# Repacking the latent-attention q, the rotary key and the delta-rule q/k norms of one long fp32 kernel

## What is computed

```python
q = q * rsqrt(sum(q*q) + eps) * 128**-0.5      # per token and head, 128 features
k = k * rsqrt(sum(k*k) + eps)
```

```python
q = (_rms_norm(c_q, q_norm) @ w_uq).reshape(B, S, 8, 96)     # c_q has 384 features
q = concatenate([q[..., :64], _rope(q[..., 64:], positions)])
k_pe = broadcast(_rope(k_rope, positions), 8 heads)          # k_rope = h @ w_kr, 32 features
_rope(t): t1, t2 = halves of 16; concat([t1*cos - t2*sin, t2*cos + t1*sin])
```

## Time and profile before

| | us |
|---|---|
| median of 3 runs (lowest, highest) | 2778.39 (2776.52, 2786.57) |
| the profiled execution, its own time | 2773.64 |
| its span in the trace | 2771.8 |
| PE, DVE, ACT, POOL busy in it | 2631.3, 1504.0, 935.1, 368.4 |

### The profile page before, as it was taken

The page is one execution under the profiler, slowest core; times in us unless marked ns, Lnnn a source line. Parts: engine busy times, 40 slices in busy tenths (PEclk is TensorE's granted clock), DMA queues, the critical chain, the costliest instruction groups (busy, mean ns, idle before and its releaser), DMA issues.

```text
span 2771.8 us, 36466 instructions
## 1 busy us (share of the span) xinstructions
PE 2631.3 (95%) x14714; PEld 1817.7 (66%) x14714; DVE 1504.0 (54%) x2935; ACT 935.1 (34%) x2234; POOL 368.4 (13%) x277
## 2 busy tenths in 40 slices
PE   6899999999999899999999899999999999999997
PEld 3567767667676576646544346677767663888886
DVE  2487786887877636534342445433475222677722
ACT  2436456465473531032342233222233212222100
POOL 0221121220221000000000121222032210000031
PEclk8999999999999999999999999999999999999999
DMA  5221321312213425121001031111322121122220
GB/s 234 76 43 45 91 60 45 81 29 83 60 44 92 134 90 218 56 99 46 15 31 38 26 100 61 61 61 61 137 76 85 52 91 61 61 91 92 84 84 31
DMA packets 108649, 209.78 MB, mean 76 GB/s; under 512 B 82433, under 2 KB 88385, under 8 KB 96961
## 3 DMA queue, kind: packets, MB, share of 16 engines
q1 hardware_dynamic: 85728, 202.37, 21.3%
q10 hardware_dynamic: 22752, 5.08, 1.0%
HBM read 195.20 MB, written 11.63 MB: 75 GB/s over the span
## 4 chain that ended last, share of the span: by engine, by line
PE 84%; DVE 6%; ACT 6%; DMA 2%; issue 1%; ACTq 0%; SPq 0%; DVEq 0%
PE ps L1420 12%; PE ps L1856 10%; PE ps L2060 9%; PE ps L1326 8%; PE ps L1621 6%; PE ps L2088 5%; PE ps L1873 3%; PE ps L2000 3%; PE ps L1743 2%; PE ps L1487 2%; PE ps L1502 2%; PE ps L1755 2%; ACT arena L2118 1%; PE ps L1729 1%; PE ps L1591 1%; PE ps L1570 1%
## 5 line engine op out<-in xcount | busy, mean ns | idle before, releaser
L2117 ACT ACTIVATE arena<-ps 64x128 f32<-64x128 f32 (+9 forms) x704 | 275.1, 408 | 754.8 <-PE ps L1856 158.6
L1420 PE MATMUL ps<-arena 128*128 128x385 f32 x1232 | 425.8, 494 | 16.1 <-ACT arena L2117 15.1
L1420 PEld LDWEIGHTS ps<-arena 128*128 128x128 f32 x1232 | 228.2, 191 | 165.3 <-POOL arena L3510 13.8
L1856 PE MATMUL ps<-arena 128*128 128x256 f32 x1456 | 327.7, 379 | 2.0 <-ACT arena L2117 2.0
L1856 PEld LDWEIGHTS ps<-arena 128*128 128x128 f32 x1456 | 270.4, 190 | 40.5 <-issue 5.7
L2060 PE MATMUL ps<-arena 128*128 128x256 f32 x1176 | 254.6, 378 | 0.0
L2060 PEld LDWEIGHTS ps<-arena 128*128 128x128 f32 x1176 | 222.1, 189 | 32.8 <-issue 0.5
L1326 PE MATMUL ps<-arena 128*128 128x512 f32 x496 | 222.2, 606 | 14.8 <-DVE arena L3168 5.1
L1326 PEld LDWEIGHTS ps<-arena 128*128 128x128 f32 x496 | 95.4, 194 | 140.1 <-issue 128.0
L2118 ACT ACTIVATE arena<-ps,arena 128x128 f32<-128x128 f32 x544 | 157.1, 378 | 45.1 <-PE ps L1555 24.2
L1621 PE MATMUL ps<-arena 128*128 128x512 f32 (+1 forms) x512 | 170.3, 487 | 0.3 <-DVE arena L2995 0.3
(11 more groups left out here) (357 smaller groups left out, 4143.7 us busy)
## 6 DMA issues: line engine op xcount, KB each, us to landing
arena<-in_ada_w SPq DMA_DIRECT2D x12, 2048.0 KB, 9.9
arena<-in_w_up SPq DMA_DIRECT2D x11, 2048.0 KB, 7.8
arena<-in_w_dil SPq DMA_DIRECT2D x9, 2048.0 KB, 7.8
arena<-in_w_dn SPq DMA_DIRECT2D x8, 2048.0 KB, 10.1
arena<-gsum SPq DMA_DIRECT2D x24, 512.0 KB, 4.9
arena<-in_w_gate SPq DMA_DIRECT2D x6, 2048.0 KB, 8.2
arena<-in_w_down SPq DMA_DIRECT2D x4, 2816.0 KB, 9.5
arena<-in_att_in SPq DMA_DIRECT2D x5, 2048.0 KB, 8.1
```

The costliest lines, as they stand in the source:

```text
L1420: m = e.matmul(ps[:, bank, 0:HALF_PAD], left[:, k], right[:, k], start=first and k == 0, stop=k == 3, skip_group_check=not first)
L1856: m = e.matmul(ps[:, bank, 0:256], left[:, k], right[:, k], start=first and k == 0, stop=k == 3, skip_group_check=not first)
L2117: return e.activation(out, x, ACT.Copy)
```

## The change

1. `dn_order`, k = 1 to 7: the steps norm q and norm k become one step `norms`, where norm q stood. On PE the ones tile has 64 columns: q's sums go to partitions 0 to 63 and k's to partitions 64 to 127 of the same banks, 6 and 7. ACT does one Ln over 768 columns and then four Exps over 64 partitions each, which spread each half over all partitions: q's into `rsA`, k's into `sqA`.
2. q of the latent attention: the columns of w_uq are reordered on the host into four tiles of the unrotated parts (two heads each) and two tiles of the rotated parts (four heads each, n = 4 and 5). PE does tiles 4, 5, 0, 1, 2, 3.
3. kr: weight tiles of 32 columns; the eight steps go in turn to four column groups (partitions 0, 32, 64, 96), two into each; a matmul with a 0/1 matrix `add32` sums the four partial results onto partitions 64 to 95 after q tile 4. The zero filling of `wkr` on POOL goes.
4. The exchange of halves: for each of q tiles 4 and 5 eight DMAs of 16 rows x 512, for the key two. The waits on an earlier rotation go; each has buffers of its own. DVE turns all 128 rows of a tile with two multiplications, and four adds write the heads' rows into `qm`. The angle tables are made on 128 rows and not 96.
5. The load of the first dilated weights now waits for q tile 3, the last one. The constants grow by 33 columns.

```diff
-                      t[17:] + [("norm", k, 0)] + zh[8:10] + z_add("P7"),
-                      [("norm_x", k, 0), ("norm", k, 1)] + zh[10:12],
+                      t[17:] + [("norms", k)] + zh[8:10] + z_add("P7"),
+                      [("norm_x", k, 0)] + zh[10:12],
@@ tensor_program
+            def norms(j):
+                for n in range(2):
+                    e.wait_ge(*at("nrm_sq", j, n))
+                take_banks(6, 7)
+                for b, a, width in ((6, 0, 512), (7, 512, 256)):
+                    for n, U in enumerate(UPPER):
+                        m = e.matmul(ps[U, b, 0:width], ones[:, 0:64], square_of(j, n)[:, a:a + width], start=True, stop=True)
@@ kr and q
-                m = e.matmul(ps[0:96, 5, :], wkr[:, k * 96:k * 96 + 96], hk(k), start=k == 0, stop=k == 7)
+                a = 32 * (k % 4)
+                m = e.matmul(ps[a:a + 32, 5, :], wkr[:, k * 32:k * 32 + 32], hk(k), start=k < 4, stop=k >= 4)
-            for h in range(8):
-                b, w = h % 4, slab("w_uq", 0)
+            for i, n in enumerate((4, 5, 0, 1, 2, 3)):
+                b, w = i % 4, slab("w_uq", 0)
                 take_banks(b)
                 for k in range(3):
-                    m = e.matmul(ps[0:96, b, :], w[:, k * 768 + h * 96:k * 768 + h * 96 + 96], cq[:, k * 512:(k + 1) * 512],
+                    m = e.matmul(ps[:, b, :], w[:, k * 768 + n * 128:k * 768 + n * 128 + 128], cq[:, k * 512:(k + 1) * 512],
+                if n == 4:
+                    e.wait_ge(*at("kr_ev", "parts"))
+                    take_banks(6)
+                    e.matmul(ps[64:96, 6, :], K("add32"), kr_parts, start=True, stop=True).then_inc(*mark("kr_pe", "sum"))
@@ scalar_program
+            def norms(j):
+                ln = oF[:, T_ALL:2 * T_ALL]
+                e.wait_ge(*at("nrm_pe", j))
+                e.activation(ln, psf[:, 3072:3072 + T_ALL], ACT.Ln, bias=eps).then_inc(*mark("nrm_ln", j))
+                for n, U in enumerate(UPPER):
+                    for to in UPPER:
+                        if n == 0:
+                            m = e.activation(rsA[to], ln[U], ACT.Exp, scale=-0.5, bias=K("lnq")[U])
+                        else:
+                            m = e.activation(sqA[to], ln[U], ACT.Exp, scale=-0.5)
@@ scalar_program, after the copies of cq and ckv
-                copy(qm[0:96, h * 512:(h + 1) * 512], ps[0:96, h % 4, :]).then_inc(*mark("uq_ev", h))
-                if h % 2:
-                    p = h // 2
-                    if p:
-                        e.wait_ge(*(at("uq_x", p - 2, 2) if p > 1 else at("kr_x", 2)))
-                    swap(qm[:, p * 1024:(p + 1) * 1024], swapped[p % 2], f"uq_swap{p % 2}_", p)
+            def swap(x, to, tag):
+                for a in range(0, x.shape[0], 32):
+                    for t in range(2):
+                        e.dma_start(to[a + 16 * t:a + 16 * t + 16], x[a + 16 - 16 * t:a + 32 - 16 * t]).then_inc(
+                            *landed(f"{tag}_swap{t}", a))
+            for i, n in enumerate((4, 5, 0, 1, 2, 3)):
+                b = i % 4
+                e.wait_ge(*at("uq_pe", n))
+                if n >= 4:
+                    copy(rope[n - 4], ps[:, b, :]).then_inc(*mark("uq_ev", n))
+                    swap(rope[n - 4], swapped[n - 4], f"uq{n - 4}")
+                else:
+                    copy(qm[0:64, 2 * n * 512:(2 * n + 1) * 512], ps[0:64, b, :])
+                    copy(qm[0:64, (2 * n + 1) * 512:(2 * n + 2) * 512], ps[64:128, b, :]).then_inc(*mark("uq_ev", n))
+                if n == 4:
+                    e.wait_ge(*at("kr_pe", "sum"))
+                    copy(kr[ROT], ps[ROT, 6, :]).then_inc(*mark("kr_ev", "sum"))
+                    swap(kr[ROT], kr_swapped[ROT], "kr")
@@ vector_program
-                e.tensor_tensor(x, x, rsA, MUL).then_inc(*mark("qk", j, n))
+                e.tensor_tensor(x, x, sqA if j and n else rsA, MUL).then_inc(*mark("qk", j, n))
+            def rotate(x, other, rows_, tag, turned, outs):
+                e.tensor_tensor(other[rows_], other[rows_], sinT[rows_], MUL)
+                e.tensor_tensor(x[rows_], x[rows_], cosT[rows_], MUL).then_inc(*mark(*turned))
+                for part, out, event in outs:
+                    e.tensor_tensor(out, x[part], other[part], ADD).then_inc(*mark(*event))
```

More of the change, by code:

```diff
@@ L177, in constants @@
     f = np.float32(10000.0) ** (-np.arange(16, dtype=np.float32) / np.float32(16))
-    invf[64:80, 0] = f
-    invf[80:96, 0] = f
+    invf[:, 0] = np.tile(f, 8)
     put("invf", invf)
+    put("sign", np.where(r % 32 < 16, -1.0, 1.0))
+    put("add32", r % 32 == np.arange(32)[None, :])
     return a
@@ L688, in program @@
         mark_e = top[0]
-        wkr, kr = take(8 * 96), take(512)
+        wkr, kr, kr_parts = take(8 * 32), take(512), take(512)
         top[0] = mark_e
@@ L693, in program @@
         PT_mla = [take(4 * 512) for _ in range(2)]
-        swapped = [arena[:, a:a + 1024] for a in (top[0], WORDS - 4096 - 1024)]
+        rope, swapped = ([arena[:, a + n:a + n + 512] for n in (0, 512)] for a in (top[0], WORDS - 4096 - 1024))
+        kr_swapped = PT_mla[0][:, 0:512]
         top[0] = mark_d
@@ L1424, in pair_product, with norm @@
                     leave_banks((f"pair_{event}", j, p), bank)
[L1426 to L1433, removed]
+            def norm(n):
+                s = square_of(0, n)
+                e.wait_ge(*at("nrm_sq", 0, n))
+                take_banks(0, 1)
+                e.matmul(ps[:, 0, :], ones, s[:, 0:512], start=True, stop=True)
+                e.matmul(ps[:, 1, 0:256], ones, s[:, 512:768], start=True, stop=True).then_inc(*mark("nrm_pe", 0, n))
+                leave_banks(("nrm_ln", 0, n), 0, 1)
+            def norms(j):
[5 more added lines that the diff above has]
+                        m = e.matmul(ps[U, b, 0:width], ones[:, 0:64], square_of(j, n)[:, a:a + width], start=True, stop=True)
+                m.then_inc(*mark("nrm_pe", j))
+                leave_banks(("nrm_ln", j), 6, 7)
             def turn(j, h):
@@ L1637, in tensor_program @@
                 elif what == "norm":
-                    norm(*which)
+                    norm(which[1])
+                elif what == "norms":
+                    norms(*which)
                 elif what == "turn":
@@ L2249, in silu, with norm @@
                 e.preload_act_table_set(LN_SET)
-            def norm(j, n):
-                e.wait_ge(*at("nrm_pe", j, n))
+            def norm(n):
+                e.wait_ge(*at("nrm_pe", 0, n))
                 if n:
[L2254 to L2259, removed]
+                    e.wait_ge(*at("qk", 0, 0))
+                e.activation(rsA, psf[:, 0:T_ALL], ACT.Ln, bias=eps).then_inc(*mark("nrm_ln", 0, n))
+                e.wait_ge(*at("nrm_ln", 0, n))
                 if n == 0:
@@ L3203, in vector_program @@
             normed("ckvn", 2, ckv, lambda k: ckv[:, k * 512:(k + 1) * 512], V("mla_kv"))
-            ROT = slice(64, 96)
-            def rotate96(x, other, name, *which):
-                n = x.shape[1] // 512
-                x, other = (y[ROT].rearrange("p (h n) -> p h n", h=n) for y in (x, other))
-                e.tensor_tensor(other, other, bc(sinT[ROT], 1, [32, n, 512]), MUL).then_inc(*mark(name, *which, 0))
-                e.tensor_tensor(x, x, bc(cosT[ROT], 1, [32, n, 512]), MUL).then_inc(*mark(name, *which, 1))
-                e.wait_ge(*at(name, *which, 0))
-                e.wait_ge(*at(name, *which, 1))
-                e.tensor_tensor(x, x, other, ADD).then_inc(*mark(name, *which, 2))
@@ L3229, in seven_adds @@
+            rotate(kr, kr_swapped, ROT, "kr", ("kr_cos",), [(ROT, kr[ROT], ("kr_x",))])
+            for r in range(2):
+                rotate(rope[r], swapped[r], slice(0, 128), f"uq{r}", ("uq_cos", r), [
+                    (slice(32 * i, 32 * i + 32), qm[ROT, (4 * r + i) * 512:(4 * r + i + 1) * 512], ("uq_x", 4 * r + i))
+                    for i in range(4)])
             def seven_adds(tag, i, p, name):
```

92 lines of the change are left out of this document (42 added, 50 removed).

## The result

The changed kernel took 2763.56 us (median of six runs, 2755.61 to 2767.48), the kernel before, beside it, 2778.27 (six runs, 2773.63 to 2786.57). The ratio is 0.9939 with a 95% interval from 0.9924 to 0.9954, so the change saves 12.8 to 21 us: 14.7 by the two medians, 17 by the ratio. The forecast was 2762.1 us from 2778.39, a ratio of 0.9941.

The account below looks back on a forecast made before the run. PE, busy for 95% of the span, was taken as the bound. Norms 9.3 us plus latent stage 7.0 us made 16.3 us, so 2778.39 us would become 2762.1 us, range 2754 to 2772.

Parts of the forecast that it names:

- The norms: Delta rounds on PE: joint norms take 1.45 us for 2.78, saving 1.33 us a round, 9.3 us over seven.
- rival A: Delta rounds: column groups take turns in the norms, so 9.3 us saved becomes 0.2; time 2771.2 us; chance 0.07.
- ACT's block: Delta rounds: ACT's Ln and four Exps take 4.46 us; the later P7 copy leaves 0.75 us cover, costing nothing.
- Rival B: Delta rounds: ACT's longer block holds up join w64, losing 6 us; time 2768 us; chance 0.11.
- The key: Latent attention's rope key on PE: 2.0 us in four column groups for 6.9, saving 4.9 us; the sum costs 1.0.
- q: Latent attention's q on PE: 36 instructions for 48 at the same 0.43 us pitch, saving 5.2 us.
- ACT's order and the wait: Latent attention: ACT's DMA issues delay its copies, so PE waits 2.4 us before uk; first score 6.4 us earlier.
- The clock: Behind the wait before uk: 2.4 us of idle lies under both known waits, 2.61 and 3.43 us; no loss.
- rival C: Before uk: a 3 us wait makes PE's clock fall, losing 6.8 us; time 2768.9 us; chance 0.12.
- DVE and POOL: Latent attention: rotations and key copies end 10 us before the score; DVE starts 0.45 us behind it; stage gains 7.0.
- Sum: Whole kernel: 9.3 us from the norms and 7.0 from the latent stage, 16.3 us saved, giving 2762.1 us.
- Rival D: Latent attention: ACT's DMA issues stall its queue and the kernel gets slower, 2794.5 us at 2.0 us an issue; chance 0.04.

Follow-up runs that it names:

- e6: Changed kernel plus a one-column matmul with 128-column weights between the norms step's two pairs; executed once, 2760.98 us; norms step 1.90 us.
- e2: Changed kernel with the two separate steps norm q and norm k put back, so the latent stage alone; 2770.17 us, ratio 0.9976 to the kernel before.
- e8: The changed kernel itself, measured again in another session; 2760.03 us against 2773.56 for the kernel before, ratio 0.9951.
- e9: Changed kernel with all eighteen exchange DMAs issued by SP and none by ACT; 2755.34 us, ratio 0.9929 to the kernel before.
- e1: Kernel before with only the norms step of the change; 2763.41 us, ratio 0.9960 to the kernel before.
- e5: Changed kernel with the norms' matmuls ordered q, q, k, k and not q, k, q, k; executed once, 2762.99 us.
- e7: Changed kernel plus a one-column matmul with 64-column weights between the norms step's two pairs; executed once, 2764.49 us; norms step 1.55 us.
- e4: Changed kernel with q tile 5's eight exchange DMAs issued on ACT after the copies of tiles 0 to 3; 2761.47 us, ratio 0.9956 to the kernel before.

## Why the prediction was right, step by step

**What bounds the kernel: right.** PE was the bound and a cut on PE came through.

**The norms: the step right, its neighbours missed.** Predicted 1.45 us, measured 1.44; rival A (the groups take turns) is out. But from the norms' start to w64 it is 210.15 - 201.59 = 8.56 us where it was 208.66 - 198.96 = 9.70: 1.14 us gained and not 1.33. The mis-sized term is the 1.39 us of a norm, which I counted as saved whole. 1.29 of it is streaming, and 0.10 is what a group with 128 columns paid for standing behind one with 64. P4 shows it in the kernel before: its row behind the join w64 begins at 210.21 and the next at 213.00, 2.79 us, where P7 and P3 behind the norms took 2.69 and 2.68. That price doesn't go with the norm. P3 now stands behind the join x64 and pays it (2.78 us to the next row for 2.68), and P7 stands behind the norms, which have 64 columns now, and pays it too (2.79 for 2.69). e6 shows such a change to cost this and more. Over the whole period of a round it is 1.19 us, 8.3 for seven and not 9.3.

**ACT's block: right.** Predicted 4.46 us, measured 207.68 - 203.15 = 4.53: half the partitions at 768 columns take the full-height time. The copy of P7 is late as computed, and the first of the copies at L2961 ends near 208.78 + 0.36 = 209.1, 1.0 us before PE reaches w64, where 0.75 were forecast. Rival B is out: no idle at w64 in any round.

**The key: right.** Predicted 2.0 us, measured 1606.41 - 1604.56 = 1.85, so the four column groups overlap, and the switches within the group cost less than I allowed. The sum took 0.98 us (0.96 forecast).

**q: right.** 36 instructions at the pitch of 48, but for the first six, which stand behind the key's 32-column weights: 1609.18 - 1606.41 = 2.77 us where six pitches of 0.43 are 2.58. It is the neighbour's price again, some 0.19 us, and the sum had no term for it.

**ACT's order and the wait: right in place, too small in size.** The wait before uk came where it was forecast and was ended by ACT's copy, but took 3.02 us and not 2.4. The mis-sized term is the issue. I priced eight of them by the pair in the earlier trace rows, 0.58 us each; in a run of eight they took 5.08 / 8 = 0.64. That put ACT's copies 0.8 us later against the key's start than forecast, and PE's q tiles 0.2.

**The clock: the step that failed, in part.** I gave rival C 0.12, since a wait of 2.4 us lay below both rows I had, 2.61 us at full speed and 3.43 with the clock lost. The wait of 3.02 us lost it, in after, e2 and e8 alike: uk took 8.74 to 8.80 us for 7.04. The window at uk's beginning, in after (columns as above):

```profile
1626.30:1630.00 3.70, 3.68 (x5) 1.69 (x6) 3.60 (x5) 1.14 (x3) 2.35 (x3) 0.55 0.92 394
```

PE is busy throughout at a granted clock of 0.55, which loses 3.7 x 0.45 = 1.7 us; from 1630 on it is 1.00 again. The price was 1.7 us and not 6.8. In the earlier trace rows PE was as busy behind its wait (17.54 of 18 us, the rest being the end of the wait) and still lost 6.8 us by the clock, four times as much. What differs is the wait, 3.43 and 3.02 us, and the work behind it, 32 columns a matmul there and 512 here; no run parts the two, so the reason is open. The length of the idle time alone doesn't decide whether the clock is lost: 1.89 us kept it in the trace of before and lost it in the ten others, 2.22 us lost it in e9, 2.61 us kept it and 2.82 lost it in e1.

**DVE and POOL: right, with a gain I missed.** The rotations and POOL's copies of the key were hidden. The last rotation ended at 1631.33, 26.8 us behind the key's start where 24.8 were forecast, and 10.45 us before the first score (10 forecast). POOL's copies, 6.5 us in the forecast, took 8.23. For the exchange, 32 KB landed in 2.0 us where 64 KB took 2.4 (medians), so most of a landing is the same for both sizes, as forecast. That DVE's first step came 0.50 us behind the score and not 1.06 was forecast (0.45). That the idle before the first probabilities' transposes would fall from 2.61 us to 1.68 was not: of these 0.93 us only 0.56 were in my sum, and the other 0.37 are DVE's step at L3152 free of POOL's sums (0.29 us for 0.67), as e9 shows from the other side.

**Sum.** First score 4.05 us earlier and not 6.4 (1.7 by the clock, 0.6 by the issues); the stage 5.0 and not 7.0; the norms 8.3 and not 9.3; in all 13.3 us for 16.3. e8's 13.5 us is this sum, and e1 and e2 hold its parts in their intervals, though their own estimates add up to 17.8. The first measurement's ratio (17 us) came nearer the forecast than its terms did, so part of the hit is luck: the three large misses (norms 1.0, clock 1.7, issues 0.6) all went the same way, the small gains that I missed (0.4 on DVE, 0.15 on the key) made up little of it, and the interval was wide enough to hide the 3 us. Whether a few microseconds more were saved outside the two places, the runs leave open. Rival D (issues that stall, slower than before) is out: the longest run of eight took 5.08 us.

## What to carry to other kernels

A small DMA between places in SBUF cost its issuing engine 0.51 to 0.64 us here, whatever its landing hides: count the issues on the engine whose copies empty the next banks, and give them to the engine with nothing behind them. Whoever takes 5 us of wait away should read next which two engines now meet: here DVE and POOL did, a half-clock stretch followed, and 2.2 of the 4.9 us were given back. When a sum of small terms is to be tested against a measurement whose interval is as wide as half the sum, run each part alone and the whole twice; single traces of the same kernel differ by 10 us.

## What the runs showed of the hardware that I had not expected

- Pairs of column halves overlap in whatever order the program has them: 1.44 us for q, k, q, k and 1.45 for q, q, k, k (e5).
- Changing from 64 to 128 columns of weights and back within a run cost 0.35 us for both (e6 less e7, the wider weight load included), and 0.10 us for a product behind a 64-column step. The Trainium skill, TensorEngine Tiling (Array Packing), Key Properties, has a change of mode drain TensorE; the rows agree that such a change has a price, and no row shows the drain itself.
- What a lost clock costs differed fourfold behind waits of nearly the same length: 1.7 us behind 3.02 us of idle (uk), 6.8 behind 3.43, with PE busy behind the wait in both.
- Exps over 64 partitions cost what they cost over 128: 0.94 and 0.84 us for 768 columns.
- The same idle time of 1.89 us at the same instruction kept TensorE at its upper clock (2.4 GHz) in the trace of before and left eight matmuls at 2.08 us for 1.23 in that of after. The other level is 1.2 GHz, and the granted clock over 95 us was 0.93 and 0.84.
- Four DVE adds of 32 x 512 took 3.12 us nearly alone and 6.34 beside POOL's additions (e4).
